# Attention probabilities turned by VectorE in 32 by 32 blocks, after GpSimd has divided them from quadrant to quadrant

## The reference

```python
s = einsum('bnqhgd,bnkhd->bnhgqk', qb, kw) * HEAD_DIM ** -0.5
s = where(valid, s + bias, -inf)              # bias by distance, |distance| <= 128
m = maximum(max(s), sink)
p = exp(s - m)
denom = sum(p) + exp(sink - m)
o = einsum('bnhgqk,bnkhd->bnqhgd', p / denom, vw)
...
x = x + concatenate([ya, yb, yc], axis=-1) @ w_out
x = x + expert_choice_ffn(rmsnorm(x), ...)
```

## Time and profile before

| | |
|---|---|
| time, median of 3 runs | 2318.82 us (2317.18 to 2319.92) |
| the profiled execution | 2318.55 us, its span 2317.1 us |
| TensorE busy | 98% of the span |
| VectorE busy | 53% |
| ScalarE busy | 27% |
| GpSimd busy | 23% |
| granted TensorE clock | 0.995 of full speed |

### The profile page before, as it was taken

One profiled execution on the slowest core, in us unless ns is written; L12 is line 12 of the kernel. 1 busy time (PEld: TensorE's weight loads), 2 busy tenths in 40 slices (PEclk: granted clock), 3 DMA queues, 4 the chain that ended last, 5 costly groups with the idle time before them and its releaser, 6 DMA issues.

```text
span 2317.1 us, 33010 instructions
## 1 busy us (share of the span) xinstructions
PE 2273.0 (98%) x12766; PEld 1613.8 (70%) x12766; DVE 1239.2 (53%) x2399; ACT 622.8 (27%) x1445; POOL 542.8 (23%) x552
## 2 busy tenths in 40 slices
PE   8999999999999999999999999999999999999998
PEld 6556587874556778887775665878755567888776
DVE  3554466586647344555236434765865463455542
ACT  3221233464332111111132212335633421111111
POOL 1003454144211111111110034532432111111111
PEclk9999999999999999999999999999999999999999
DMA  4002132221127988878530111312212279888883
GB/s 155 21 25 68 55 122 74 74 91 56 74 73 254 348 302 292 299 264 284 148 120 21 37 55 59 119 60 82 83 55 82 82 274 343 300 290 274 284 295 83
DMA packets 149653, 352.16 MB, mean 152 GB/s; under 512 B 9941, under 2 KB 38105, under 8 KB 149498
## 3 DMA queue, kind: packets, MB, share of 16 engines
q1 hardware_dynamic: 134234, 308.11, 37.1%
q0 software_dynamic: 15264, 41.95, 7.4%
HBM read 307.75 MB, written 42.28 MB: 151 GB/s over the span
## 4 chain that ended last, share of the span: by engine, by line
PE 93%; DVE 4%; DMA 1%; ACT 1%; issue 1%; POOL 0%; SPq 0%; DVEq 0%; ACTq 0%; POOLq 0%
PE ps L1842 89%; PE ps L2127 1%; PE ps L2188 1%; DVE HT L1784 1%; PE ps L1861 1%; DVE TMP L1248 1%; DMA HT<-h_sample,idxs 0%; PE ps L1894 0%; DVE HT L1248 0%; PE ps L2139 0%; DVE TMP L1257 0%; ACT SCR L1051 0%; DMA MID<-w_in 0%; DVE SCR L1248 0%; POOL SCR L753 0%
## 5 line engine op out<-in xcount | busy, mean ns | idle before, releaser
L1842 PE MATMUL ps<-MID,HT 128*128 128x512 f32 (+3 forms) x2560 | 694.2, 491 | 4.8 <-DMA MID<-w_in 3.0
L1842 PEld LDWEIGHTS ps<-HT,MID 128*128 128x128 f32 x4096 | 557.2, 191 | 16.4 <-issue 15.4
L1842 PE MATMUL ps<-HT,MID 128*128 128x160 f32 (+1 forms) x4096 | 560.5, 299 | 1.0 <-DVE HT L1248 0.9
L1842 PEld LDWEIGHTS ps<-MID,HT 128*128 128x128 f32 (+1 forms) x2560 | 293.7, 157 | 248.3 <-issue 207.7
L1842 PE MATMUL ps<-RING,HT 128*128 128x256 f32 (+2 forms) x1760 | 395.8, 392 | 1.7 <-DVE RING L1252 1.3
L1842 PEld LDWEIGHTS ps<-RING,HT 128*128 128x128 f32 (+1 forms) x1760 | 310.7, 189 | 83.5 <-issue 40.7
L1842 PE MATMUL ps<-HT,RING 128*128 128x512 f32 (+1 forms) x960 | 350.0, 522 | 0.0
L1842 PEld LDWEIGHTS ps<-HT,RING 128*128 128x128 f32 x960 | 180.2, 190 | 157.8 <-issue 149.8
L1784 DVE STREAM_TRANSPOSE HT<-HT 32x256 f32<-32x256 f32 x576 | 251.0, 436 | 18.3
L1257 DVE SCALAR_TENSOR_TENSOR HT<-HT,ps 128x160 f32<-128x160 f32 (+1 forms) x128 | 40.9, 319 | 397.1 <-ACT HT L1210 395.1
L850 POOL DMA_INDIRECT y_prompt<-SCR,idxp x32 | 50.5, 1578 | 583.1 <-ACT SCR L1220 562.2
(11 more groups left out here) (268 smaller groups left out, 2177.2 us busy)
## 6 DMA issues: line engine op xcount, KB each, us to landing
MID<-w_gate SPq DMA_DIRECT2D x32, 2048.0 KB, 9.4
MID<-w_up SPq DMA_DIRECT2D x32, 2048.0 KB, 15.0
MID<-w_down SPq DMA_DIRECT2D x32, 2048.0 KB, 16.2
RING<-w_in SPq DMA_DIRECT2D x20, 1024.0 KB, 5.3
SCR<-cs_rows SPq DMA_DIRECT2D x20, 1024.0 KB, 5.2
MID<-w_out SPq DMA_DIRECT2D x8, 1024.0 KB, 6.4
y_sample<-RING SPq DMA_DIRECT2D x16, 512.0 KB, 2.6
h_sample<-HT SPq DMA_DIRECT2D x16, 512.0 KB, 2.6
```

Of the source, the lines that this page charges most:

```text
L1842: return pe.matmul(out, a, b, start=start, stop=stop)
```

## The change

For chunks 2 to 9 the probabilities are no longer transposed by TensorE. The scores come out of the matmul in another order of keys: within a head first the quadrant b of the key (32 of 128), then the block k, then i. `attn_scale` is now 16 multiplications of 32 partitions each: it reads the quadrant a of the queries and the part b of the keys and writes to the partitions of quadrant b of a new tile PB. One VectorE instruction (four, where there are two blocks of keys) then transposes PB in blocks of 32 by 32 into PT, where the keys are on partitions and the queries on the free axis. It stands between `keep_h2(n - 1, 1)` and `keep_y(n + 1, 1)`. ScalarE's copies `keep_p` and TensorE's `turn_p` stay for chunks 0 and 1 alone. The bias table is kept in the new order of keys: its DMA goes to a staging tile in the mLSTM part of layer 0 and GpSimd copies it into place in four instructions; the two loads of `w_out` that use that space move from the mLSTM chunks 3 and 4 to 6 and 7. For chunks 0 and 1 the addition of the bias becomes two instructions instead of one.

```diff
                     def attn_scale(n):
-                        nk, c0 = attn_keys(ORDER[n])
+                        w = 32 * attn_keys(ORDER[n])[0]
                         pool.wait_ge(r_made, n + 1)
-                        v = PSC[n % 2][:, :, 0:nk * P]
-                        link(pool.tensor_tensor(v, v, ADEN[n % 2].unsqueeze(2).to_broadcast([P, AH, nk * P]), ALU.mult), pn_made)
+                        if n < 2:
+                            v = PSN[n][:, :, 0:4 * w]
+                            link(pool.tensor_tensor(v, v, ADEN[n].unsqueeze(2).to_broadcast([P, AH, 4 * w]), ALU.mult), pn_made)
+                            return
+                        v = PSC[n % 2][:, :, :, 0:w]
+                        if n >= 3:
+                            pool.wait_ge(p_turned, 2 * AH + n - 2)
+                        for a in range(4):
+                            at = slice(32 * a, 32 * a + 32)
+                            for b in range(4):
+                                link(pool.tensor_tensor(PB[32 * b:32 * b + 32, a, :, 0:w], v[at, b],
+                                                        ADEN[n % 2][at].unsqueeze(2).to_broadcast([32, AH, w]), ALU.mult),
+                                     pn_made if a == b == 3 else pool_chain, wait=a == b == 3)
...
+                        if layer == 0 and c == 3:
+                            pool.wait_ge(hot_loaded, 48)
+                            for h in range(AH):
+                                link(pool.tensor_copy(bia[:, h].rearrange("p b (k i) -> p b k i", k=3),
+                                                      STAGE[:, h][:, ::-1].rearrange("p (k b i) -> p b k i", k=3, b=4)))
...
+                    def turn_p(n):
+                        nk, c0 = attn_keys(ORDER[n])
+                        dve.wait_ge(pn_made, n + 1)
+                        dve.wait_ge(o_made, n)
+                        out = PT.rearrange("p (h k a j) -> p a h k j", h=AH, k=3, a=4)[:, :, :, 0:nk, :]
+                        if nk == 3:
+                            link(dve.transpose(out.rearrange("p a h k j -> p a (h k) j"), PB.rearrange("p a h (k i) -> p a (h k) i", k=3)), p_turned)
+                            return
+                        for a in range(4):
+                            turned = link(dve.transpose(out[:, a], PB[:, a, :, 0:32 * nk].rearrange("p h (k i) -> p h k i", k=nk)),
+                                          p_turned if a == 3 else dve_chain, wait=a == 3)
...
                         take_x(n)
                         keep_h2(n - 1, 1)
+                        turn_p(n + 1)
                         keep_y(n + 1, 1)
...
                     route(n - 1)
+                    turn_p(n + 1)
                     dve.wait_ge(aff_turned, 1)
                     rounds(0, 15)
...
-                        keep_p(n + 1)
+                        if n == 0:
+                            keep_p(1)
...
-                            pe.wait_ge(p_kept, AH * (n + 1))
+                            if n < 2:
+                                pe.wait_ge(p_kept, AH * (n + 1))
+                            else:
+                                pe.wait_ge(p_turned, 2 * AH + n - 1)
```

More of the change, by code:

```diff
@@ L212, in program @@
         PT = VO[:, 0:AH * 384]
-        PSC = [SCR[:, 1536 * b:1536 * (b + 1)].rearrange("p (h k) -> p h k", h=AH) for b in range(2)]
+        PSCF = [SCR[:, 1536 * b:1536 * (b + 1)] for b in range(2)]
+        PSC = [a.rearrange("p (b h x) -> p b h x", b=4, h=AH) for a in PSCF]
+        PSN = [a.rearrange("p (h k) -> p h k", h=AH) for a in PSCF]
+        PBF = HT[:, 8704:8704 + 4 * AH * 96]
+        PB = PBF.rearrange("p (a h x) -> p a h x", a=4, h=AH)
+        STAGE = MID[:, bc_at:bc_at + AH * 384].rearrange("p (h k) -> p h k", h=AH)
         ident, tri = cstt[:, 0:P], [cstt[:, P:2 * P], cstt[:, 2 * P:3 * P]]
         ones1 = cstt[:, 3 * P:3 * P + 1]
-        bia = bias[:, :].rearrange("p (h k) -> p h k", h=AH)
+        bia = bias[:, :].rearrange("p (h b x) -> p h b x", h=AH, b=4)
         EW = [MID[:, j * 12288:(j + 1) * 12288] for j in range(2)]
@@ L609, in _ @@
                         m_load(c)
-                        if c in (3, 4):
-                            k = 2 * c - 4
+                        if layer == 0 and c == 2:
+                            sp.wait_ge(hot_loaded, 32)
+                            sp.wait_ge(wk_made, 2 * len(STEPS))
+                            sp.dma_start(STAGE, bass.AP(tensor=btab.tensor, offset=0, ap=[[1, P], [512, AH], [1, 384]])).then_inc(hot_loaded, 16)
+                        if c in (6, 7):
+                            if layer == 0 and c == 6:
+                                sp.wait_ge(md_masked, 2 * 6 + 1)
+                            k = 2 * c - 10
                             sp.dma_start(WO[k], wo_rows[:, k:k + 2]).then_inc(wo_loaded, 16)
@@ L1560, in attn_shift @@
                         if n >= 2 and j == 0:
-                            dve.wait_ge(p_turned, AH * (n - 1))
-                        v = PSC[n % 2][:, j:AH:2, 0:nk * P]
+                            if n < 4:
+                                dve.wait_ge(p_turned, AH * (n - 1))
+                            else:
+                                dve.wait_ge(pn_made, n - 1)
                         b = 6 if (n, j) == (0, 1) else 4
-                        tt(v, ps[:, b:b + 2, 0:nk * P], bia[:, j:AH:2, b1 - nk * P:b1][:, :, ::-1], ALU.add, s_read)
-                        link(dve.tensor_reduce(out=m[:, j:AH:2], in_=v, axis=AX, op=ALU.max))
+                        if n < 2:
+                            v = PSN[n][:, j:AH:2, 0:nk * P]
+                            for q in range(2):
+                                h = j + 2 * q
+                                link(dve.tensor_tensor(PSN[n][:, h, 0:nk * P].rearrange("p (k b i) -> p b k i", b=4, i=32),
+                                                       ps[:, b + q, 0:nk * P].rearrange("p (k b i) -> p b k i", b=4, i=32),
+                                                       bia[:, h, :, at:at + w].rearrange("p b (k i) -> p b k i", i=32), ALU.add),
+                                     s_read if q else dve_chain)
+                        else:
+                            v = PSC[n % 2][:, :, j:AH:2, 0:w].rearrange("p b h x -> p h b x")
+                            tt(v, ps[:, b:b + 2, 0:nk * P].rearrange("p h (b x) -> p h b x", b=4), bia[:, j:AH:2, :, at:at + w], ALU.add, s_read)
+                        link(dve.tensor_reduce(out=m[:, j:AH:2], in_=v, axis=mybir.AxisListType.XY if n >= 2 else AX, op=ALU.max))
                         if j == 1:
@@ L2126, in turn_p @@
                         for b in range(nk):
-                            last = pe.transpose(ps[:, 6 + h % 2, b * P:(b + 1) * P], PSC[n % 2][:, h, b * P:(b + 1) * P], ident)
+                            last = pe.transpose(ps[:, 6 + h % 2, b * P:(b + 1) * P], PSN[n][:, h, b * P:(b + 1) * P], ident)
                         last.then_inc(p_turned, 1)
```

40 lines of the change are left out of this document (10 added, 30 removed).

## The result

The changed kernel takes 2333.2 us (median; 2331.29 to 2333.76) against 2318.53 (2317.18 to 2319.92) for the kernel before on the same chip: a ratio of 1.0062, 95% interval 1.0044 to 1.0079. The forecast was 2333.9. In the profiled executions the span grew from 2317.1 to 2331.8 us, by 14.7.

What follows compares the result with a forecast made beforehand. TensorE, 98% busy, bounds the kernel; VectorE, 1.03 us behind, would set the rounds. Per layer +0.6 + 2.3 + 3.1 + 1.5 = 7.5 us, 15 for two, on 2318.55: 2333.9 us, range 2320 to 2348.

Steps and rivals of the forecast that it cites:

- A block is worth 0.11 us: TensorE, attention loop: each removed 128x128 transpose saves 0.11 us, 84 blocks or 9.2 us a layer.
- VectorE's transpose, 1.80 with its gap: VectorE ahead of keep_y(n + 1, 1): transposing 1536 elements takes 1.74 us, 1.80 with wait and gap.
- Steady round 21.63: Rounds 2 to 4: TensorE waits 1.5 us for VectorE at the product; 21.63 us against 21.42, +0.21 each.
- GpSimd's ring, 19.9: GpSimd's pieces, root, then scale_out and exponentials on ScalarE, until the next pieces: 19.9 us, under the round's 21.6.
- Rounds 6 and 7, +0.15: Rounds with two key blocks: four short VectorE transposes, 1.84 us with gaps, make each round 0.15 us longer.
- Pieces at 0.86 with the gap: GpSimd's attn_scale: each of 16 pieces of 384 elements takes 0.82 us plus a 0.04 gap, 13.8 us together.
- First product +2.3: First round: pieces, transpose and keep_y in sequence start the product at 556.4 instead of 554.10, +2.3 us.
- the 0.6 for the split bias additions: First round, VectorE: bias additions of chunks 0 and 1, split in two, delay attn_scale(2) by 0.6 us.
- The lock, +3.1 a layer: VectorE instructions with two SBUF inputs, chiefly ml_output's five, each wait one GpSimd piece, 0.8 us: +3.1 a layer, ends 0 and 6.
- The end, +1.5: End of loop: root_out(8) behind chunk 9's pieces, and the transpose ahead of the choice, make it 1.5 us later.
- Nothing for the scores' keys in runs of 32: Scores' matmul on TensorE: reading keys in runs of 32 charged nothing, end +0.2 us a call.
- Rival 1: No lock to speak of between VectorE and GpSimd, the rest as forecast: 2327.7 us, chance 0.15.

Runs made afterwards that it cites:

- the fastest version: Changed kernel with chunks 0, 1, 2, 9 the old way, half of keep_h2 on ScalarE, ml_output in round 1, take_x behind keep_y(n+1, 1): 2307.82 us.
- the control: Kernel before, transposes on TensorE, plus only ml_output in round 1, take_x behind keep_y(n+1, 1) and half of keep_h2 on ScalarE: 2318.42 us.
- the one with both edits: Changed kernel with chunks 0, 1, 2 and 9 the old way and the second half of keep_h2 on ScalarE: 2312.29 us, ratio 0.9975.
- the two moves in the changed kernel: Changed kernel in full, with ml_output moved to round 1 and take_x behind keep_y(n+1, 1) on VectorE: 2325.43 us, ratio 1.0032.

## Why the prediction came out right

**Step by step.**

- *A block is worth 0.11 us.* Held: where nothing else binds, in rounds 2 and 3 of the fastest version, a round takes 20.10 us against 21.41, which is the 1.32 of 12 blocks.
- *VectorE's transpose, 1.80 with its gap.* 1.78 busy, 1.70 from start to start. *Steady round 21.63.* It is 21.53, with 1.36 us of idle time instead of 1.5. The mechanism and the size held: the run with one piece shows that GpSimd has no part in a round of this length, those with a short transpose and with moved instructions that it is as long as VectorE's stretch makes it.
- *GpSimd's ring, 19.9.* Too short: with 14.5 for the pieces instead of 13.8 the same sum gives 20.6, and 20.4 to 20.6 is what the traces show. It doesn't touch the steady round of the changed kernel, as I said, but it holds VectorE up behind the first product (by 0.73 us at attn_den(4) in layer 1), and it is what limits the fastest version.
- *Rounds 6 and 7, +0.15.* Wrong sign, -0.34. The term is the transpose of two key blocks: I took 4 x 0.436 from the earlier trace rows, whose instructions of 32 partitions start 0.47 us apart (eight take 3.71); the new ones of 128 partitions start 0.34 apart, and four take 1.43 us. Why they follow more closely is not shown. With 1.40 for 1.84 the same sum gives -0.29.
- *Pieces at 0.86 with the gap.* 16 took 14.59 us, 0.91 each. *First product +2.3.* It is +2.36, but by two misses that nearly cancel: the pieces took 0.8 us more, and the 0.6 for the split bias additions never came (attn_scale(2) starts 14.14 us behind turn_y(0, 2), 14.15 before).
- *The lock, +3.1 a layer.* Mis-sized: +0.68 in layer 0 and 1.24 in layer 1. ml_output grew by 1.5 us against its time without pieces, not 4.0, and scores(5, 1) was 0.61 and 1.18 us late, not 2.6. This is the step that failed most; the price per instruction came from one row of 2.00 us, the wait for a piece of 2.75. A short piece in the way costs on average a part of itself. Nor is this term the lock alone: the two layers differ because attn_den(4) waits for the ring in layer 1 and not in layer 0, and with the clock kept the round takes 1.3 us more than a steady one in both.
- *The end, +1.5.* The choice starts 14.61 us behind round 7's product (698.96 - 684.35), where I had 14.6, again by two misses that cancel: route ends at 13.22 instead of 12.75, and the transposes hold the choice up for 1.4 instead of 1.84. In layer 1 VectorE set the time and it cost 1.1; in layer 0 the clock cost more.
- *Nothing for the scores' keys in runs of 32.* Held: four matmuls take 0.92 us as before.
- *What I had not seen:* the clock. A long idle time ahead of the first product followed from my sum, but not that TensorE comes back from it slower: 2.1 and 1.5 us over a steady round, of which the kept clock gave back 1.0 and 0.9. At the end of layer 0 it happened once more (granted clock 0.91 from 700 to 708, where before had 1.00): from the transposition of the affinities to the product of chunk 9 there are 9.81 us, in layer 1 8.11 for the same instructions at 1.00. The idle times just ahead are the same in both layers (0.43 and 1.67 us), so what decides this fall is not shown; in the run with idle matmuls it came in layer 1 instead.

By the distances in the table, the lock was 2.1 us a layer too dear, the excess behind the first product, which I had not seen, was 1.8 a layer, and the short transposes gave 1.0: the loops cost 12.1 us and not 15.0. Rival 1, no lock to speak of, was nearer to the size of that term (0.7 and 1.2 us) than the forecast of 3.1. So the mechanism of the rounds was right, and that the total came within 1 us is luck: the errors cancel, and the part outside the loops fills up the rest.

**The part outside the loops is not shown to be the change's.** Of the 3.2 us between the layers, 2.6 lie in one place, where TensorE waits for ScalarE at the start of layer 1. Before, then after:

```profile
1160.71 6.34 PE L1842 MATMUL ps<-MID,HT 128*128 128x288 f32 x16 [0.95 <-DVE HT L1248]
...
1170.07 1.09 PE L1861 MATMUL ps<-cstt,MID 128*128 128x128 f32 x8 [1.92 <-ACT MID L888]
1171.00 4.05 PE L1842 MATMUL ps<-MID,HT 128*128 128x288 f32 x16
```

```profile
1167.98 4.12 PE L1889 MATMUL ps<-MID,HT 128*128 128x288 f32 x16 [1.24 <-DVE HT L1269]
...
1177.34 1.97 PE L1908 MATMUL ps<-cstt,MID 128*128 128x128 f32 x8 [4.14 <-ACT MID L911]
1179.10 5.86 PE L1889 MATMUL ps<-MID,HT 128*128 128x288 f32 x16
```

The wait ends 9.36 us behind the first row in both. Before, the slow matmuls lie ahead of it and are hidden by it; after, they lie behind it. Which of the two it is does not follow the change alone: the control, which has none of it, and the run with keep_h2 ahead of scale_out, which has all of it, show the first pattern (959.0 and 959.1 us from the one loop to the other, 958.7 before), while the runs with one piece and with chunks 2 and 9 undone show the second (961.8 for the latter, 961.9 in the changed kernel). Other runs lie between or beyond (the one with both edits 959.1, the two moves in the changed kernel 962.4), and of the two traces without the change none has the second pattern, so a part of the change in it is not ruled out. What decides it was not found. So some 3 us of a single trace here are weak evidence on a kernel.

## What to carry to other kernels

Work taken from a busy engine is paid out only up to the next engine's chain: look at the shortest slack (here 1.03 us of VectorE, against 1.70 put into its chain and 0.66 of TensorE's work removed beside it, which gives the idle time of 1.36 to within 0.03), and shorten that chain in the same edit, by moving out of it what nobody needs yet. Leave out of the new path the first and the last item of a loop, where its latency is bare. Here the two together turned +0.6% into -0.4%. Then work out the ring behind that chain too: GpSimd's 20.5 us was hidden at 21.5 and binds at 20.1. And when a wait grows to several microseconds, look at TensorE's clock behind it.

## What the runs showed of the hardware

- After 5.36 us without a matmul the granted clock of TensorE was 0.55 over the next 5 us, and the product behind it took 2.83 us; behind 3.39 us of idle time (the changed kernel with the two moves) it took 2.61 in one layer and 2.83 in the other. Idle times of 1.36 us in every round left the product at 1.53. After 0.43 and 1.67 us of idle time at the end of a layer the granted clock was 0.79 over 8 us in layer 0 and 1.00 in layer 1. Idle matmuls in the gap kept the clock at 1.00.
- GpSimd writes 32 partitions of one quadrant to another at the price of their length, 841 ns for 384 elements and 607 for 256, and 16 back to back take 0.91 us each for 384. The 4 pieces of a chunk that stay in their quadrant are in the same rows and not told apart.
- VectorE's instructions on SBUF data take at most 0.67 us longer beside pieces of 0.91 than without (one of 8 elements 0.83 us instead of 0.17, one of 512 with two inputs 0.97 instead of 0.69), and go in between two pieces; additions from PSUM keep their 0.69.
